# Retention's rotation split between two engines: GpSimd turns the queries, VectorE the keys

## The chip, the cores and the metric

One core of a Trainium2 chip runs the kernel. The core has five engines with instruction streams of their own (TensorE for matmuls, VectorE, ScalarE and GpSimd for elementwise work, SyncE for issuing transfers) and 16 DMA engines. They meet through semaphores only. The metric is the time of one execution on the device in microseconds; times within the trace count from the start of the span.

## The reference

The program is two blocks of two layers each, on 256 rows of width 1024. The second block is the one that matters here. In each of its layers the normalized rows are projected to queries, keys and values of a retention branch, to the features of an RWKV-7 branch (a recurrence over time, computed in chunks), to a pooling branch and to gates:

```python
def rotary(x, positions):
    half = x.shape[-1] // 2
    freqs = ROPE_BASE ** (-jnp.arange(half, dtype=jnp.float32) / half)
    ang = positions.astype(jnp.float32)[..., None] * freqs
    cos = jnp.cos(ang)[:, :, None, :]
    sin = jnp.sin(ang)[:, :, None, :]
    x32 = x.astype(jnp.float32)
    x1, x2 = x32[..., :half], x32[..., half:]
    return jnp.concatenate([x1 * cos - x2 * sin, x1 * sin + x2 * cos], axis=-1)
...
    qh = rotary(q.reshape(B, T, H, dh), positions)
    kh = rotary(k.reshape(B, T, H, dh), positions) * (dh ** -0.5)
...
    scores = jnp.einsum('bhnid,bhnjd->bhnij', qc, kc) * decay_mask[None, :, None]
```

With 4 heads of 128, both queries and keys are 256 rows of 512 numbers. The rotation is elementwise: each number is multiplied by a cosine and its partner by a sine, and the two products are subtracted or added.

## The kernel before

All weights stream through the core. Each projection is a piece of 128x2048 numbers, loaded by SyncE into a ring of three. ScalarE rounds a piece to its high half (`part0h` or `part1h`, two buffers in turn) and the low half (`part0l`, `part1l`) is the difference, made by VectorE for most pieces (line 1453, in two operations of 128x1024) and by GpSimd for some (line 3020). TensorE multiplies each piece in three passes, high by high, high by low and low by high, 48 matmuls for a projection, and waits for the first and for the second low half apart (`low_half`). The pieces of the second block go in the order `rw6 rw0 ... rw5 rq0 rq1 rk0 rk1 u0 u1 rv0 rv1 rg0 rg1 pg0 pg1 ...`, where `rq`, `rk` and `rv` are the retention's queries, keys and values, and `rg` its gate.

Nothing schedules at run time: each engine has its program in a written order. In a layer of the second block, `prepare` first does the features of the recurrence and then, from a list of jobs that all engines step through with `jobs.fill()`, the projections of the other branches between its own steps. On VectorE `prepare` ends with the scaled operands of the recurrence, `AR` (line 2257), `bt_` (line 2260) and the scaled keys `kt_` (line 2263), and then `jobs.fill()` makes the low half of `rg0`. On TensorE `prepare` turns (transposes) `vN` and `bkN` from these, multiplies `rg0`, does the pooling, waits for the signal `rot` and turns the rotated queries and keys (line 621).

The rotation before the change is GpSimd's: `rotate`, called behind the job `rk1`, runs over queries and keys and the two tiles of 128 rows. For each tile it makes four products of 128x256 into the tile `grow`, waits for them, and writes a difference and a sum back into the rows. `grow` later holds a gate row, which ScalarE writes behind the same signal `rot`.

Of the kernel before, what the change touches and what calls it, by code (L numbers as in the profile page):

```python
# [10 lines left out]
ALU = mybir.AluOpType  # L11
# [216 lines left out]
def v(ap, **k):  # L228
    names = list(k)
    return ap.rearrange("p (" + " ".join(names) + ") -> p " + " ".join(names), **{a: b for a, b in k.items() if b})  # L230
# [1207 lines left out]
def vector_program(w, K):  # L1438
    e, M, V, ps, at, done = w.e, K.mem, K.vector, K.psum, K.at, K.done
# [23 lines left out]
    def bank(*name):  # L1463
        w.wait_ge(*done[name if len(name) > 1 else name[0]])
        return ps[name]
# [706 lines left out]
    def headnorm_end(banks, name, n, d, dsts):  # L2172
# [7 lines left out]
            last = e.tensor_tensor(dst, dst, rv[:, k * n:k * n + n].unsqueeze(2).to_broadcast([128, n, d]), ALU.mult)  # L2180
        return last

    def prepare(l, jobs):
        Z = M.Z[l]
        V.mark("v", "begin", l)
# [8 lines left out]
        for j in (6, 0, 1, 2, 3, 4, 5):  # L2194
# [18 lines left out]
            if j == 4:  # L2213
                t = bank("ksum", l)
                e.tensor_scalar(Z.n8, t[0:8, 0:256], 1e-24, None, ALU.max).then_inc(*V("n8 in", l))
                ps.free(("ksum", l), V.now())
        for cp in range(2):
            t = bank("kn", cp, l)
# [42 lines left out]
        w.wait_ge(*at["kd", l])  # L2261
        w.wait_ge(*V.now())
        e.tensor_tensor(kt, k4, ee, ALU.mult).then_inc(*V("k", l))
        jobs.fill()
        V.mark("v", "ph2", l)
        jobs.fill()
# [2 lines left out]
        t = bank("pool", 1, l)  # L2269
        e.tensor_copy(Z.dT[:, 2:4, :], v(t[:, :], c=2, n=256)).then_inc(*V("dT", 1, l))  # L2270
        ps.free(("pool", 1, l), V.now())
        for i in range(2):
            t = bank("kT", i, l)
# [7 lines left out]
        for cp in range(2):  # L2281
            t = bank("bon", cp, l)
# [4 lines left out]
        for h in range(4):  # L2287
            t = bank("ST", h, l)
# [11 lines left out]
        for gp in range(2):  # L2300
            t = bank("pw", gp, l)
# [7 lines left out]
        for cp in range(2):  # L2309
            t = bank("yT", cp, l)  # L2310
# [169 lines left out]
    for l in range(L):  # L2480
        jobs = Jobs(jobs2(), lambda name: job2(l, name))
        prepare(l, jobs)
        norms = []
        for i in range(2):
            chunk(l, i, jobs, norms)
        turn_y(l, 1)
        V.mark("v", "end2", l)
        rwkv_low(l, 1)
        V.mark("A2", l, 0)
        V.mark("A2", l, 1)  # L2490
        jobs.rest()
        for j in range(4):
            merge(l, 2, j)
            if j == 1:
                split_to(PIECE[l, "out1"])
        for j in range(4):
            use(l, f"out{j}")
        for ch in range(2):
            combine(l, 0, ch)
        sum_squares(l + 1, 0)  # L2500
        if l < L - 1:
            scale_rows(l + 1, 0)
            split_to(PIECE[l + 1, "rw6"])
        combine(l, 1, 0)
        if l == L - 1:
            finish(0)
        combine(l, 1, 1)
        if l < L - 1:
            enter(l + 1)
# [495 lines left out]
def gpsimd_program(w, K):  # L3005
    e, M, G, ps, at, done, A, here = w.e, K.mem, K.gpsimd, K.psum, K.at, K.done, K.A, K.here
# [15 lines left out]
    def use(l, key):  # L3022
        split_to(ahead(PIECE[l, key]))

    def use_half(l, name):
        key, m = name.split(".")
        split_to(PIECE[l, key] + 1 + int(m))
# [93 lines left out]
        for q in "vs":  # L3121
            w.wait_ge(*at[q, what, l])

    def rotate(l):
        Z = M.Z[l]
        a, b = (v(M.grow[:, 512 * k:512 * k + 512], h=4, s=2, d=64) for k in range(2))
        w.wait_ge(*at["cs"])
        for src, n in ((Z.rq3, "rq"), (Z.rk3, "rk")):
            w.wait_ge(*at[n + "0", l])
            w.wait_ge(*at[n + "1", l])  # L3130
            for i in range(2):
                s4 = src[:, i, :].rearrange("p (h s d) -> p h s d", h=4, s=2)
                w.wait_ge(*G.now())
                for s in range(2):
                    e.tensor_tensor(a[:, :, s, :], s4[:, :, s, :], M.cs[:, 0, i, :].unsqueeze(1).to_broadcast([128, 4, 64]),
                                    ALU.mult).then_inc(*G())
                    e.tensor_tensor(b[:, :, s, :], s4[:, :, s, :], M.cs[:, 1, i, :].unsqueeze(1).to_broadcast([128, 4, 64]),
                                    ALU.mult).then_inc(*G())
                w.wait_ge(*G.now())
                e.tensor_tensor(s4[:, :, 0, :], a[:, :, 0, :], b[:, :, 1, :], ALU.subtract).then_inc(*G())  # L3140
                e.tensor_tensor(s4[:, :, 1, :], b[:, :, 0, :], a[:, :, 1, :], ALU.add).then_inc(*G("rot", l))

    def job2(l, name):
        if "." in name:
            use_half(l, name)
        else:
            use(l, name)
        if name == "rk1":
            rotate(l)

    def headnorm(nh, *name):
        w.wait_ge(*at["hvar", *name])
# [2 lines left out]
    for l in range(L):  # L3155
        Z = M.Z[l]
        jobs = Jobs(jobs2(), lambda name: job2(l, name))
        G.mark("g", "begin", l)
        if l == 0:
# [135 lines left out]
def build(nc, A, out):  # L3295
    with ExitStack() as ctx:
        K = Engines(nc, ctx, A, out)
        for program in (tensor_program, vector_program, scalar_program, gpsimd_program, sync_program):
            program(Port(Count()), K)
        K.at, K.done = ({k: a for k, a in t.items() if a[0] is not None} for t in (K.at, K.done))  # L3300
        K.restart()
        block = ctx.enter_context(nc.Block())

        @block.tensor
        def _(e):
            tensor_program(Port(e), K)

        @block.vector
        def _(e):
            vector_program(Port(e), K)  # L3310

        @block.scalar
        def _(e):
            scalar_program(Port(e), K)

        @block.gpsimd
        def _(e):
            gpsimd_program(Port(e), K)

        @block.sync  # L3320
        def _(e):
            sync_program(Port(e), K)
# [203 lines left out]
```

## Time and profile before

| | |
|---|---|
| median of 3 runs | 1578.39 us (1576.77, 1578.39, 1582.22) |
| the profiled execution | 1582.88 us |
| its span | 1581.0 us |
| mean granted TensorE clock | 0.996 |
| busy: TensorE, VectorE, ScalarE, GpSimd | 97%, 64%, 45%, 36% |

The span is what the profiler's records cover; the execution is 1.9 us longer. Busy shares are averages over the whole span, in which the four layers have different limits, and an engine that isn't the limit costs nothing by being idle. In the rows below, `Z` stands for the layer's own buffers (among them the retention's rows), `cs` for cosines and sines, `ps` for a PSUM bank.

### The profile page before, as it was taken

To read this page: it belongs to the slowest core of one execution; us is meant where nothing else is said; L and a number is where in the kernel's file an instruction comes from. 1 tells how busy PE (TensorE), PEld (TensorE's weight loads), DVE (VectorE), ACT (ScalarE), POOL (GpSimd) and SP (SyncE) were. 2 spreads that over 40 slices of the span, in tenths; PEclk is the share of its full clock that TensorE was granted. 3 is DMA by queue.
4 is the path that set the end of the run, shared out by engine and by line. 5 is a ranking of instruction groups with operands and counts; after the bars stand their busy time and mean duration, and the time that the engine had idled before them with its cause. 6 is when DMAs were issued, how large, how long until landed. Compare 5 with 4: busy or idle time off the path is not lost.

```text
span 1581.0 us, 35399 instructions
## 1 busy us (share of the span) xinstructions
PE 1538.2 (97%) x15704; PEld 1414.6 (89%) x15704; DVE 1005.7 (64%) x1637; ACT 712.1 (45%) x1126; POOL 563.0 (36%) x452
## 2 busy tenths in 40 slices
PE   9999999999999999999999999999999999999998
PEld 8989987899978989987999989999998899999887
DVE  4364386878784445576777786766446777764356
ACT  4554534544445455435444444633332555433223
POOL 3745613000217745503000310734673006446640
PEclk9999999999999999999999999999999999999999
DMA  9433364787545423474676545453333354533332
GB/s 357 169 122 108 113 232 191 265 299 273 187 166 211 161 89 125 161 279 187 250 283 240 204 142 182 152 176 133 135 136 135 124 197 153 182 133 138 114 130 93
DMA packets 43944, 281.49 MB, mean 178 GB/s; under 512 B 5144, under 2 KB 5272, under 8 KB 14352
## 3 DMA queue, kind: packets, MB, share of 16 engines
q1 hardware_dynamic: 42192, 270.13, 47.4%
q0 software_dynamic: 1600, 9.10, 1.5%
q8 instruction: 123, 2.02, 0.5%
q14 instruction: 29, 0.24, 0.0%
HBM read 278.15 MB, written 1.06 MB: 177 GB/s over the span
## 4 chain that ended last, share of the span: by engine, by line
PE 78%; DVE 13%; ACT 3%; issue 3%; POOL 2%; DMA 0%; POOLq 0%; SPq 0%; ACTq 0%; DVEq 0%
PE ps L613 75%; DVE part0l L1453 3%; DVE part1l L1453 3%; PE ps L621 3%; ACT part0h L2523 1%; DVE rows L1890 1%; ACT part1h L2523 1%; DVE Pr L1887 1%; ACT gates L2520 1%; ACT Xh L2523 1%; DVE Xl L1468 1%; DVE small L1484 0%; DMA ring<-in_w 0%; DVE raw L2012 0%; DVE mgx L2144 0%
## 5 line engine op out<-in xcount | busy, mean ns | idle before, releaser
L2523 ACT ACTIVATE part1h<-ring 128x1024 fp32r<-128x1024 f32 (+1 forms) x216 | 215.8, 1047 | 226.0 <-PE ps L613 213.6
L2523 ACT ACTIVATE part0h<-ring 128x1024 fp32r<-128x1024 f32 (+1 forms) x216 | 213.0, 1035 | 209.6 <-PE ps L613 194.3
L613 PE MATMUL ps<-Xh,part1h 128*128 128x256 f32 x968 | 276.7, 286 | 7.5 <-DVE Xl L1468 2.4
L613 PE MATMUL ps<-Xh,part0h 128*128 128x256 f32 (+1 forms) x952 | 270.9, 285 | 3.4 <-DVE Xl L1468 1.3
L613 PE MATMUL ps<-Xl,part1h 128*128 128x256 f32 x968 | 271.1, 280 | 0.0
L613 PE MATMUL ps<-Xh,part1l 128*128 128x256 f32 x968 | 270.9, 280 | 0.0
L613 PE MATMUL ps<-Xl,part0h 128*128 128x256 f32 (+1 forms) x952 | 265.2, 279 | 0.0
L613 PE MATMUL ps<-Xh,part0l 128*128 128x256 f32 (+1 forms) x952 | 265.1, 278 | 0.0
L3020 POOL TENSOR_TENSOR part1l<-ring,part1h 128x512 fp32r<-128x512 f32 x144 | 185.3, 1317 | 102.5 <-ACT part1h L2523 102.3
L3020 POOL TENSOR_TENSOR part0l<-ring,part0h 128x512 fp32r<-128x512 f32 x144 | 185.3, 1318 | 101.8 <-ACT part0h L2523 101.7
L1453 DVE TENSOR_TENSOR part1l<-ring,part1h 128x1024 fp32r<-128x1024 f32 (+1 forms) x144 | 181.3, 1299 | 52.3 <-ACT part1h L2523 52.0
L1453 DVE TENSOR_TENSOR part0l<-ring,part0h 128x1024 fp32r<-128x1024 f32 (+1 forms) x144 | 178.0, 1277 | 54.2 <-ACT part0h L2523 54.1
L613 PEld LDWEIGHTS ps<-Xh,part1h 128*128 128x128 f32 x968 | 183.7, 190 | 12.1 <-DVE Xl L1468 4.0
L613 PEld LDWEIGHTS ps<-Xh,part0h 128*128 128x128 f32 (+1 forms) x952 | 178.4, 187 | 7.9 <-DVE Xl L1468 2.3
L613 PEld LDWEIGHTS ps<-Xl,part1h 128*128 128x128 f32 x968 | 184.2, 190 | 1.1 <-issue 0.9
L613 PEld LDWEIGHTS ps<-Xh,part1l 128*128 128x128 f32 x968 | 183.8, 190 | 0.0
L613 PEld LDWEIGHTS ps<-Xl,part0h 128*128 128x128 f32 (+1 forms) x952 | 178.8, 188 | 1.6 <-issue 1.3
L613 PEld LDWEIGHTS ps<-Xh,part0l 128*128 128x128 f32 (+1 forms) x952 | 178.2, 187 | 0.0
L3058 POOL TENSOR_TENSOR x<-xh,rows 128x512 f32<-128x512 f32 x20 | 32.6, 1630 | 321.7 <-DVE hid L2002 284.5
L613 PE MATMUL ps<-part1h,Xh 128*128 128x256 f32 (+1 forms) x256 | 79.7, 311 | 2.9 <-DVE part1l L1453 2.3
L613 PE MATMUL ps<-part0h,Xh 128*128 128x256 f32 (+1 forms) x256 | 79.6, 311 | 2.3 <-DVE part0l L1453 1.7
L613 PE MATMUL ps<-part1l,Xh 128*128 128x256 f32 (+1 forms) x256 | 78.4, 306 | 0.0
(446 smaller groups left out, 3260.4 us busy)
## 6 DMA issues: line engine op xcount, KB each, us to landing
ring<-in_w SPq DMA_DIRECT2D x211, 1024.0 KB, 4.9
hid<-in_ada SPq DMA_DIRECT2D x36, 512.0 KB, 6.3
hid<-in_w SPq DMA_DIRECT2D x6, 1024.0 KB, 11.1
rows<-in_lnrow POOLq DMA_DIRECT2D x6, 1024.0 KB, 9.9
fqk<-in_ada SPq DMA_DIRECT2D x6, 512.0 KB, 6.1
cq<-in_ada SPq DMA_DIRECT2D x6, 512.0 KB, 6.5
gates<-in_c SPq DMA_DIRECT2D x2, 1536.0 KB, 9.5
ring<-in_w SPq DMA_DIRECT2D x4, 512.0 KB, 5.6
```

The costliest lines, as they stand in the source:

```text
L613: return e.matmul(o, a, b, start=st, stop=sp)
L621: return e.transpose(o, a, ident[0:a.shape[0], 0:a.shape[0]])
L1453: e.tensor_tensor(lo[:, h * c:h * c + c], raw[:, h * c:h * c + c], f32(hi[:, h * c:h * c + c]), ALU.subtract).then_inc(*V("low", m, h))
L1468: return e.tensor_tensor(hl[1], raw, f32(hl[0]), ALU.subtract).then_inc(*V(*name))
L1887: e.scalar_tensor_tensor(out=tmp, in0=g, scalar=1.0, in1=t[:, :], op0=ALU.add, op1=ALU.mult).then_inc(*V())
L1890: e.tensor_tensor(m, m, tmp, ALU.add).then_inc(*V("merged", bq, j, l))
L2520: return e.activation(o, a, f, **k)
L2523: return e.activation(o, a, ACT.Copy)
L3020: e.tensor_tensor(lo[:, o], raw[:, o], f32(hi[:, o]), ALU.subtract).then_inc(*G("low", m, h))
L3058: e.tensor_tensor(x3[:, i, c], xh3[:, i, c], M.rows[:, c], ALU.mult).then_inc(*G())
```

## The change

The rotation of the keys goes from GpSimd to VectorE. GpSimd's part, `rotate_queries`, is what `rotate` did for the queries, and ends with a signal of its own. VectorE's part, `rotate_keys`, stands directly behind the scaled keys (`kt_`) and ahead of the job that makes the low half of `rg0`. It waits for the queries first, since both use `grow`. It takes each product in one operation over 128x512 in place of two over 128x256, so a tile of rows needs 4 operations in place of 6, and it gives the signal `rot`.

```diff
@@ vector_program
+    def rotate_keys(l):
+        Z = M.Z[l]
+        a, b = (M.grow[:, 512 * k:512 * k + 512] for k in range(2))
+        a8, b8 = (t.rearrange("p (x d) -> p x d", d=64) for t in (a, b))
+        a4, b4 = (v(t, h=4, s=2, d=64) for t in (a, b))
+        w.wait_ge(*at["cs"])
+        w.wait_ge(*at["turned queries", l])
+        w.wait_ge(*at["rk0", l])
+        w.wait_ge(*at["rk1", l])
+        for i in range(2):
+            s8 = Z.rk3[:, i, :].rearrange("p (x d) -> p x d", d=64)
+            s4 = Z.rk3[:, i, :].rearrange("p (h s d) -> p h s d", h=4, s=2)
+            w.wait_ge(*V.now())
+            for t8, cs in ((a8, 0), (b8, 1)):
+                e.tensor_tensor(t8, s8, M.cs[:, cs, i, :].unsqueeze(1).to_broadcast([128, 8, 64]), ALU.mult).then_inc(*V())
+            w.wait_ge(*V.now())
+            e.tensor_tensor(s4[:, :, 0, :], a4[:, :, 0, :], b4[:, :, 1, :], ALU.subtract).then_inc(*V())
+            e.tensor_tensor(s4[:, :, 1, :], b4[:, :, 0, :], a4[:, :, 1, :], ALU.add).then_inc(*V("rot", l))
+
     def prepare(l, jobs):
...
         e.tensor_tensor(kt, k4, ee, ALU.mult).then_inc(*V("k", l))
+        rotate_keys(l)
         jobs.fill()
         V.mark("v", "ph2", l)
@@ gpsimd_program
-    def rotate(l):
+    def rotate_queries(l):
...
-        for src, n in ((Z.rq3, "rq"), (Z.rk3, "rk")):
-            w.wait_ge(*at[n + "0", l])
-            w.wait_ge(*at[n + "1", l])
-            for i in range(2):
-                s4 = src[:, i, :].rearrange("p (h s d) -> p h s d", h=4, s=2)
...
+        w.wait_ge(*at["rq0", l])
+        w.wait_ge(*at["rq1", l])
+        for i in range(2):
+            s4 = Z.rq3[:, i, :].rearrange("p (h s d) -> p h s d", h=4, s=2)
...
+            e.tensor_tensor(s4[:, :, 1, :], b[:, :, 0, :], a[:, :, 1, :], ALU.add).then_inc(*G("turned queries", l))
...
-        if name == "rk1":
-            rotate(l)
+        if name == "rk0":
+            rotate_queries(l)
```

VectorE in the first layer of the second block, from the scaled operands of the recurrence to the low halves of `rg0` and `rg1`, before:

```order
L2257 SCALAR_TENSOR_TENSOR AR<-gates,bt_ 128x8x128
L2260 TENSOR_TENSOR bt_<-kt_,Z 128x1024
L2263 TENSOR_TENSOR kt_<-gates,Z 128x1024
L1453 TENSOR_TENSOR part1l<-ring,part1h 128x1024 x2
L1453 TENSOR_TENSOR part0l<-ring,part0h 128x1024 x2
```

and after:

```order
L2276 SCALAR_TENSOR_TENSOR AR<-gates,bt_ 128x8x128
L2279 TENSOR_TENSOR bt_<-kt_,Z 128x1024
L2282 TENSOR_TENSOR kt_<-gates,Z 128x1024
L2197 TENSOR_TENSOR grow<-Z,cs 128x512 x2
L2199 TENSOR_TENSOR Z<-grow 128x4x64
L2200 TENSOR_TENSOR Z<-grow 128x4x64
L2197 TENSOR_TENSOR grow<-Z,cs 128x512 x2
L2199 TENSOR_TENSOR Z<-grow 128x4x64
L2200 TENSOR_TENSOR Z<-grow 128x4x64
L1453 TENSOR_TENSOR part1l<-ring,part1h 128x1024 x2
L1453 TENSOR_TENSOR part0l<-ring,part0h 128x1024 x2
```

Eight operations now stand between the scaled keys and the first low half of `rg0`; the rest of VectorE's order is the same.

GpSimd at the end of the rotation, the last tile of the keys and what follows it (a memset of the recurrence's masked scores), before:

```order
L3135 TENSOR_TENSOR grow<-Z,cs 128x4x64
L3137 TENSOR_TENSOR grow<-Z,cs 128x4x64
L3135 TENSOR_TENSOR grow<-Z,cs 128x4x64
L3137 TENSOR_TENSOR grow<-Z,cs 128x4x64
L3140 TENSOR_TENSOR Z<-grow 128x4x64
L3141 TENSOR_TENSOR Z<-grow 128x4x64
L3190 MEMSET Z 128x2048
```

and after, where it is the last tile of the queries:

```order
L3154 TENSOR_TENSOR grow<-Z,cs 128x4x64
L3156 TENSOR_TENSOR grow<-Z,cs 128x4x64
L3154 TENSOR_TENSOR grow<-Z,cs 128x4x64
L3156 TENSOR_TENSOR grow<-Z,cs 128x4x64
L3159 TENSOR_TENSOR Z<-grow 128x4x64
L3160 TENSOR_TENSOR Z<-grow 128x4x64
L3209 MEMSET Z 128x2048
```

The pattern is the same; it stands two times in a layer instead of four. The orders of TensorE, ScalarE and SyncE are unchanged.

## Rows read from the trace of the kernel before

**Rows 1.** Page, part 1: busy time of each engine, share and instructions.

```profile
PE 1538.2 (97%) x15704; PEld 1414.6 (89%) x15704; DVE 1005.7 (64%) x1637; ACT 712.1 (45%) x1126; POOL 563.0 (36%) x452
```

**Rows 2.** Page, part 4: engines' shares of the chain that ended last.

```profile
PE 78%; DVE 13%; ACT 3%; issue 3%; POOL 2%; DMA 0%; POOLq 0%; SPq 0%; ACTq 0%; DVEq 0%
```

**Rows 3.** Waits of TensorE, 945 to 1100: total us, times, longest.

```profile
PE ps L613 <- DVE part0l L1453: 1.5, 2, 1.0
PE ps L613 <- DVE part1l L1453: 0.6, 2, 0.4
```

**Rows 4.** Timeline of GpSimd, 925 to 1110: start, us, engine, line, what.

```profile
1005.69 1.52 POOL L3135 TENSOR_TENSOR grow<-Z,cs 128x256 f32<-128x256 f32 x1
...
1022.00 0.74 POOL L3141 TENSOR_TENSOR Z<-grow 128x256 f32<-128x256 f32 x1
1022.91 0.74 POOL L3135 TENSOR_TENSOR grow<-Z,cs 128x256 f32<-128x256 f32 x1 [0.17 <-POOL Z L3141]
...
1039.39 0.73 POOL L3141 TENSOR_TENSOR Z<-grow 128x256 f32<-128x256 f32 x1
```

**Rows 5.** Timeline of VectorE, 945 to 1100, around the scaled keys.

```profile
1024.00 3.11 DVE L1453 TENSOR_TENSOR part0l<-ring,part0h 128x1024 fp32r<-128x1024 f32 x2 [2.56 <-ACT part0h L2523]
1027.14 1.64 DVE L2257 SCALAR_TENSOR_TENSOR AR<-gates,bt_ 128x1024 f32<-128x1024 f32 x1
1028.82 1.65 DVE L2260 TENSOR_TENSOR bt_<-kt_,Z 128x1024 f32<-128x1024 f32 x1
1030.57 1.57 DVE L2263 TENSOR_TENSOR kt_<-gates,Z 128x1024 f32<-128x1024 f32 x1
1032.07 3.42 DVE L1453 TENSOR_TENSOR part1l<-ring,part1h 128x1024 fp32r<-128x1024 f32 x2
```

**Rows 6.** VectorE by line and shape: busy us, mean ns, idle before.

```profile
L1453 DVE TENSOR_TENSOR part1l<-ring,part1h 128x1024 fp32r<-128x1024 f32 x2 | 2.4, 1218 | 0.0
L2229 DVE TENSOR_TENSOR kt_<-bt_,gates 128x1024 f32<-128x1024 f32 x1 | 1.2, 1227 | 0.1
L2202 DVE TENSOR_TENSOR gates<-Z 128x512 f32<-128x512 f32 x6 | 4.2, 692 | 9.9 <-ACT Z L2523 9.9
L2220 DVE TENSOR_TENSOR bt_<-bt_,ps 128x512 f32<-128x512 f32 x2 | 1.3, 682 | 0.0
L2391 DVE TENSOR_TENSOR Z<-ps,c 128x256 f32<-128x256 f32 x2 | 0.8, 420 | 1.5 <-PE ps L613 1.5
```

**Rows 7.** Timeline of TensorE: the first matmuls of `rv1` and `rg0`.

```profile
1025.58 0.36 PE L613 MATMUL ps<-part0h,Xh 128*128 128x256 f32 x1 [0.99 <-DVE part0l L1453]
...
1033.96 0.36 PE L613 MATMUL ps<-Xh,part1h 128*128 128x256 f32 x1 [0.38 <-DVE part1l L1453]
```

**Rows 8.** The chain that ended last, 1000 to 1060: start, us, what.

```profile
1034.90 0.83 issue
1035.73 7.61 PE ps L613 x66
1043.35 1.75 PE ps L621 x16
```

**Rows 9.** Second layer: the chain at `rg0`; GpSimd's last operation.

```profile
1354.69 8.62 PE ps L613 x72
...
1360.13 0.73 POOL L3141 TENSOR_TENSOR Z<-grow 128x256 f32<-128x256 f32 x1
```

**Rows 10.** Timeline of TensorE: the first matmuls behind three long waits.

```profile
498.71 0.58 PE L613 MATMUL ps<-Xh,part1h 128*128 128x256 f32 x1 [2.27 <-POOL part1l L3020]
...
1217.61 0.36 PE L613 MATMUL ps<-A0h,part1h 128*128 128x256 f32 x1 [1.74 <-DVE A0l L1468]
...
1538.67 0.36 PE L613 MATMUL ps<-A1h,part0h 128*128 128x256 f32 x1 [1.94 <-DVE A1l L1468]
```

**Rows 11.** Stretches behind two of them: us, TensorE busy (matmuls), granted clock, DMA.

```profile
498.60:502.00 3.40, 3.29 (x15) 0.50 0.00 0
1217.60:1220.60 3.00, 2.99 (x26) 1.00 0.03 5
```

More of the change, by code:

```diff
@@ L3127, in rotate @@
         w.wait_ge(*at["cs"])
-        for src, n in ((Z.rq3, "rq"), (Z.rk3, "rk")):
-            w.wait_ge(*at[n + "0", l])
-            w.wait_ge(*at[n + "1", l])
-            for i in range(2):
-                s4 = src[:, i, :].rearrange("p (h s d) -> p h s d", h=4, s=2)
[L3133 to L3141, printed above, removed]
+        w.wait_ge(*at["rq0", l])
+        w.wait_ge(*at["rq1", l])
+        for i in range(2):
+            s4 = Z.rq3[:, i, :].rearrange("p (h s d) -> p h s d", h=4, s=2)
+            w.wait_ge(*G.now())
+            for s in range(2):
+                e.tensor_tensor(a[:, :, s, :], s4[:, :, s, :], M.cs[:, 0, i, :].unsqueeze(1).to_broadcast([128, 4, 64]),
+                                ALU.mult).then_inc(*G())
+                e.tensor_tensor(b[:, :, s, :], s4[:, :, s, :], M.cs[:, 1, i, :].unsqueeze(1).to_broadcast([128, 4, 64]),
+                                ALU.mult).then_inc(*G())
+            w.wait_ge(*G.now())
+            e.tensor_tensor(s4[:, :, 0, :], a[:, :, 0, :], b[:, :, 1, :], ALU.subtract).then_inc(*G())
+            e.tensor_tensor(s4[:, :, 1, :], b[:, :, 0, :], a[:, :, 1, :], ALU.add).then_inc(*G("turned queries", l))
     def job2(l, name):
```

## Prediction

> **What bounds the kernel now.** I read the page first. TensorE is busy 97% of the span [rows 1], and the chain that ended last is 78% TensorE and 13% VectorE [rows 2]. So only what makes TensorE wait, or slows it, can move the end. Next, the waits of TensorE around the retention of the first layer: 1.5 us for `part0l` and 0.6 us for `part1l` [rows 3]. These are the low halves of the split weights, which VectorE writes. No wait for GpSimd stands among them.
>
> Then GpSimd's own row of work. Its rotation runs from 1005.69 to 1040.12: 12 instructions for the queries to 1022.74, 12 for the keys from 1022.91 on [rows 4]. TensorE comes to the turning of the rows only at 1043.35 [rows 8], 3.2 us after the rotation's end. In the second layer the rotation ends at 1360.86 and the turning begins at 1363.31 [rows 9], 2.4 us later. The rotation's end is off the path in both layers; ending it earlier gives nothing by itself.
>
> What does stand on the path there is VectorE: `AR`, `bt_`, `kt_` and then the low half of `rg0`, one behind another from 1024.00 to 1035.49 [rows 5]. TensorE waited 0.99 us for the low half of `rv1` and 0.38 us for the first half of `rg0` [rows 7]. The change puts new work into exactly this row, ahead of the low half of `rg0`.
>
> **What it removes.** 12 GpSimd instructions a layer, 17.2 us of them [rows 4]. Nobody waits for them, so that alone is worth 0. But while they ran VectorE was slow: a 128x1024 operation with both inputs in SBUF took 1.64, 1.65 and 1.57 us and the pair for one piece 3.11 and 3.42 us [rows 5]; with GpSimd idle the same operation takes 1.227 us and the low half 1.218 each [rows 6], a pair about 2.36 us, since the second starts a little before the first ends. From 1022.74 on GpSimd will now be idle. So, from 1024.00: pair 2.36 instead of 3.11, three operations at 1.23 instead of 1.64, 1.65, 1.57. That is 0.75 + 0.41 + 0.42 + 0.34 = 1.9 us. `kt_` is ready at 1030.2 instead of 1032.1. The queries' rotation is not moved: the job in front of it now bears the name of another piece, but GpSimd comes to it at 1005.69 either way.
>
> The Trainium skill (SBUF — State Buffer, section Who interferes with whom) says that a VectorE instruction with two SBUF inputs contends with a GpSimd instruction that reads SBUF. By that rule the release is complete; the trace agrees, 1.227 us alone and about 1.65 us beside GpSimd.
>
> **What it adds.** Per layer 4 products of 128x512 and 4 sums of 128x256 on VectorE. A 128x512 of this kind takes 0.692 us, two in a row 1.28 us (0.682 each, overlapping), a 128x256 takes 0.42 us [rows 6], two about 0.8. With some 0.04 us for each wait on its own result (the distance from one operation to the next in rows 5) one tile of rows costs 0.04 + 1.28 + 0.04 + 0.82 = 2.2 us, both 4.4. The bounds: 4.0 if sums overlap fully, 5.7 if each ran as slowly as beside GpSimd (1.65/1.23 = 1.34 times). I take 4.4, since GpSimd is idle there. The new wait for the queries is open: they end at 1022.7, VectorE asks at 1030.2, so it costs 0 and has 7.5 us in hand. Queued behind the rotation on VectorE are the low halves of `rg0` and `rg1`. For the first TensorE waits; the second is needed 6 us later and is hidden behind `rg0`'s 48 matmuls, as now.
>
> **The sum.** Rotation from 1030.3 to 1034.7; the first low half of `rg0` 1.23 us, to 1035.95; TensorE starts 0.14 us behind it, near 1036.1. Before it started at 1033.96 [rows 7]: 2.1 us later. Two things take some back. In the first layer TensorE stood another 0.83 us without an engine to blame, within `rg0` [rows 8]; I count it as fetching of instructions, which the longer wait will cover: 2.1 - 0.8 = 1.3 us. In the second layer no such gap stands [rows 9], but the second low half came 1.71 us behind the first (half of 3.42 us), while its 12 first matmuls take 1.4 us (26 in 3.00 us [rows 11]); now it comes 1.13 us behind and is in time: 2.1 - 0.3 = 1.8 us. Together 3.1 us, bounds 1.5 (rotation 4.0, gaps wholly covered) and 6 (rotation 5.7, nothing covered).
>
> **What the longer wait does to TensorE's clock.** TensorE ends its small matmuls for `vN` and `bkN` at 1033.6 now (0.38 us ahead of 1033.96 [rows 7]), and at 1033.2 then, for `rv1` starts 0.35 us earlier. From there to 1036.1 it will stand 2.9 us, in each layer; no wait of this trace is that long. The two longest are 2.27 us and 1.94 us [rows 10]. Right behind the first the granted clock was 0.50 for 3.40 us: 15 matmuls, against 26 in 3.00 us at 1.00 behind a wait of 1.74 us [rows 10, 11]. Fifteen matmuls at the full rate take 1.73 us, so the fall from 2.4 to 1.2 GHz cost 3.40 - 1.73 = 1.7 us; a little less if part of it falls within the wait. I take 1.6 us. Bounds: 0 (no fall, as behind 1.74 us) to 3.4 (it lasts twice as long). Waits of 2.9 us lie beyond the ones that brought the fall, so I expect it in both layers: 3.2 us.
>
> The Trainium skill (TensorE: Matmul & The Clock Gate, section What's actually happening) has it that the throttled state is the default and activity releases it, so that an idle TensorE goes back to 1.2 GHz. By that rule both waits end in the low clock; the trace agrees at 2.27 us, and at 1.74 us it shows no fall.
>
> **Total.** 3.1 + 3.2 = 6.3 us. The profiled execution took 1582.88 us (span 1581.0 and 1.9 around it), so a like one of the changed kernel comes to 1589.2. The median of the runs shown is 4.5 us below the profiled one; the change adds the same to it: 1578.4 + 6.3 = 1584.7 us. What a measurement of this kernel can tell from no change is about 0.3%, 4.7 us.
>
> **Rivals.**
> 1. The waits come but the clock falls in one layer only or in none. For it: 1.74 us left the clock up, and where a fall begins is not the kernel's to choose. Against: 2.9 us is well above both waits that had it. Price 3.1 to 4.7 us: 1581.5 to 1583.1, mostly within 0.3%.
> 2. VectorE isn't given back its speed, because something other than GpSimd made it slow (the transfers of that stretch). Then `kt_` stays at 1032.1, the rotation ends at 1036.6 and TensorE waits 4 us a layer: 1.9 x 2 = 3.8 us more than my sum, 1588.5. Against: the same kind of operation is at 1.227 us 15 us later, once GpSimd is idle [rows 6].
> 3. Not slower, rather a little faster: the release outweighs the rotation. TensorE's waits of 0.99 and 0.38 us in each layer and the 0.83 us gap were born of VectorE's slow stretch; if all went it would be 0.99 + 0.38 + 0.83 + 0.99 + 0.38 = 3.6 us, 1574.8. The one mechanism is a rotation short enough to fit into what GpSimd gives back: it decides below about 1.5 us between `kt_` and the low half (1.9 us won, 0.4 lost to TensorE's readiness). For it: VectorE wins 1.9 us ahead and another 1.1 us (3.42 to 2.36) behind. Against: 8 instructions cannot be under 4.0 us by rows 6, and what is won behind the low half of `rg0` comes too late for it.
> 4. The change shortens a path that I think is open, TensorE's wait for the rotated rows. It would be 5 us earlier (1040.1 to 1034.7), but TensorE is not there before 1043: no gain, and the rest of my sum remains. If the late low half were then taken up by a later wait, the time would be 1578 to 1580. Against: no later wait of that stretch is for anything but VectorE's work behind TensorE itself.
>
> **How the numbers follow.** Forecast 0.55; rival 1 0.27; rival 2 0.08; rival 3 0.05; rival 4 0.05. Slower by over 0.3%: the forecast with 6.3 us lies 1.6 us above the bound, and I give it 0.85 of its chance, 0.47; of rival 1 a quarter, 0.07; rival 2, 0.08; together 0.62. Faster by over 0.3% needs 4.7 us, more than rival 3's whole price; I leave 0.03 to it for the scatter of the runs. Within 0.3%: 0.35. The range: the low end below rival 1 without a fall by what three runs scatter (they span 5.4 us), 1578.5; the high end at rival 2 without going beyond it, 1588.5. The forecast's own range is 1582.5 to 1587.
>
> **What would show it.** Right: on VectorE `AR`, `bt_` and `kt_` at 1.23 us each and `kt_` ending near 1030.2; 8 instructions of rotation in 4.4 us behind it; TensorE waiting about 2.9 us for the low half of `rg0` in both layers; the granted clock at 0.50 for some 3.4 us right behind; GpSimd idle from 1022.7 to its memset behind 1052; the turning of the rows still not waiting for the rotation. Wrong: a wait of TensorE below 1.5 us there (rotation or release mis-sized), a clock that stays at 1.00 (then 3 us), VectorE at 1.65 us without GpSimd beside it, or TensorE waiting less elsewhere by what it waits more here.

## The result, and the profile after

The changed kernel takes 1583.72 us (median of 15 runs, 1581.92 to 1587.72), the kernel before 1579.05 us in the same comparison (15 runs, 1575.59 to 1582.22). The ratio is 1.003, with a 95% interval of 1.0022 to 1.0038: 4.7 us slower, and clear of no change. The forecast was 6.3 us slower and 1584.7 us. The profiled execution of the changed kernel took 1583.84 us, only 1.0 us more than that of before: the clock fell at other places in the one than in the other (near 1482 and 1540 before, near 12 and 1036 after), so traces are compared stretch by stretch, and times by medians.

The timeline of VectorE in the changed kernel, first layer, from `rv1`'s low half (columns: start, us, engine, line, what; compare [rows 5]):

```profile
1023.16 2.36 DVE L1453 TENSOR_TENSOR part0l<-ring,part0h 128x1024 fp32r<-128x1024 f32 x2 [2.56 <-ACT part0h L2543]
1025.55 1.22 DVE L2276 SCALAR_TENSOR_TENSOR AR<-gates,bt_ 128x1024 f32<-128x1024 f32 x1
1026.81 1.23 DVE L2279 TENSOR_TENSOR bt_<-kt_,Z 128x1024 f32<-128x1024 f32 x1
1028.14 1.22 DVE L2282 TENSOR_TENSOR kt_<-gates,Z 128x1024 f32<-128x1024 f32 x1
1029.47 1.29 DVE L2197 TENSOR_TENSOR grow<-Z,cs 128x512 f32<-128x512 f32 x2
1030.80 0.42 DVE L2199 TENSOR_TENSOR Z<-grow 128x256 f32<-128x256 f32 x1
1031.14 0.42 DVE L2200 TENSOR_TENSOR Z<-grow 128x256 f32<-128x256 f32 x1
...
1033.60 2.35 DVE L1453 TENSOR_TENSOR part1l<-ring,part1h 128x1024 fp32r<-128x1024 f32 x2
```

This whole trace stands 0.84 us earlier here than that of before. From the start of `rv1`'s low half to the end of `kt_` it is 6.20 us now and was 8.14: GpSimd's retreat gave 1.9 us. Between `kt_` and `rg0`'s low half the rotation puts 4.2 us.

GpSimd's timeline, the last operation of the queries and the next one ([rows 4] went on to 1040.12):

```profile
1021.16 0.74 POOL L3160 TENSOR_TENSOR Z<-grow 128x256 f32<-128x256 f32 x1
1053.94 1.80 POOL L3209 MEMSET Z<- 128x2048 f32 x1 [32.04 <-PE ps L613]
```

TensorE's first matmul of `rg0` in the first and in the second layer, to be read against [rows 7]:

```profile
1034.96 0.36 PE L613 MATMUL ps<-Xh,part1h 128*128 128x256 f32 x1 [2.50 <-DVE part1l L1453]
...
1358.45 0.36 PE L613 MATMUL ps<-Xh,part0h 128*128 128x256 f32 x1 [2.70 <-DVE part0l L1453]
```

0.38 us of waiting in each layer has become 2.50 and 2.70. The gap of 0.83 us within `rg0` [rows 8] is gone: the chain has all matmuls from `rg0` to the turning as one piece (start, us, what):

```profile
1033.68 1.15 DVE part1l L1453
1034.83 0.14 issue
1034.96 10.00 PE ps L613 x72
1044.96 1.75 PE ps L621 x16
```

And the granted clock, in stretches ahead of and behind both waits (length, busy us and count of TensorE, of its weight loads, VectorE, ScalarE, GpSimd, then clock, DMA share, GB/s):

```profile
1032.50:1034.90 2.40, 0.00 (x0) 0.00 (x0) 2.37 (x5) 2.40 (x5) 0.00 (x0) 1.00 0.64 265
...
1036.50:1039.00 2.50, 2.50 (x14) 2.50 (x13) 1.72 (x2) 0.00 (x0) 0.00 (x0) 0.50 0.78 242
...
1358.50:1362.00 3.50, 3.50 (x31) 3.50 (x32) 3.21 (x3) 0.32 (x1) 0.00 (x0) 1.00 0.42 114
```

Behind the wait of the first layer the clock fell to 1.2 GHz, 14 matmuls in 2.50 us; behind that of the second it stayed at 2.4 GHz.

To compare traces I use one distance: from VectorE's start on `rv1`'s low half to TensorE's start on the turning. It holds all that the change does between, and no fall elsewhere.

| kernel | first layer | second layer |
|---|---|---|
| before | 19.18 us | 18.42 us |
| changed | 21.64 (clock fell) | 20.03 |
| difference | +2.46 | +1.61 |

### The profile page after: what moved, and what is told of

Read it like the earlier page. It is cut to its first block, busy times and chain, and to the rows that moved or that the text cites. A ratio compares the mean times of both kernels' runs of the same rounds, so it can differ in the third digit from the quotient of the medians.

```text
span 1581.9 us, 35389 instructions
## 1 busy us (share of the span) xinstructions
PE 1535.9 (97%) x15704; PEld 1413.7 (89%) x15704; DVE 1005.9 (64%) x1653; ACT 712.1 (45%) x1126; POOL 529.4 (33%) x428
## 4 chain that ended last, share of the span: by engine, by line
PE 77%; DVE 14%; ACT 4%; issue 3%; POOL 2%; DMA 0%; POOLq 0%; SPq 0%; DVEq 0%; ACTq 0%
PE ps L613 75%; DVE part0l L1453 3%; DVE part1l L1453 3%; PE ps L621 3%; ACT part0h L2543 1%; DVE rows L1890 1%; DVE mgx L2144 1%; ACT part1h L2543 1%; ACT Xh L2543 1%; DVE Xl L1468 1%; DVE Pr L1887 1%; ACT gates L2540 1%; DVE mt L2140 0%; DVE small L1484 0%; DMA ring<-in_w 0%
## 5 line engine op out<-in xcount | busy, mean ns | idle before, releaser
L613 PE MATMUL ps<-part0l,Xh 128*128 128x256 f32 (+1 forms) x256 | 78.4, 306 | 0.0
```

Of the source, the lines that this page charges most:

```text
L613: return e.matmul(o, a, b, start=st, stop=sp)
```

## The experiments

Each edit is to the changed kernel unless another is named.

**The rotation behind the low half of `rg0`.**

```diff
         e.tensor_tensor(kt, k4, ee, ALU.mult).then_inc(*V("k", l))
-        rotate_keys(l)
         jobs.fill()
+        rotate_keys(l)
```

> The keys' rotation stays on VectorE, but stands behind the low half of rg0 instead of ahead of it. Theory (the rotation costs because it stands in the row that ends in rg0's low half): TensorE no longer waits there, also not the 0.38 us of before, and the clock does not fall; about 1.2 us in the first layer and 0.7 us in the second are won against before: 1577 us, 6 to 7 us below the changed kernel. Rival (what counts is the work added to VectorE, 4.2 us a layer, wherever it stands): 1582 to 1584 us, and TensorE waits somewhere else, for the low half of rg1 or for the rotated rows.

Measured: 1578.38 us, before 1578.87, ratio 0.9999 (0.999 to 1.0009). VectorE's timeline in it, first layer:

```profile
1029.30 1.23 DVE L2282 TENSOR_TENSOR kt_<-gates,Z 128x1024 f32<-128x1024 f32 x1
1030.44 2.35 DVE L1453 TENSOR_TENSOR part1l<-ring,part1h 128x1024 fp32r<-128x1024 f32 x2
1032.90 1.29 DVE L2197 TENSOR_TENSOR grow<-Z,cs 128x512 f32<-128x512 f32 x2
...
1036.69 0.42 DVE L2200 TENSOR_TENSOR Z<-grow 128x256 f32<-128x256 f32 x1
1037.03 2.35 DVE L1453 TENSOR_TENSOR part0l<-ring,part0h 128x1024 fp32r<-128x1024 f32 x2
```

The same 8 operations cost nothing against before here, so the place was what cost 4.7 us, not the work; the rival is out. The rotation ends at 1037.1 and TensorE turns at 1042.51. The distance is 18.19 and 17.30 us, 1.0 and 1.1 us below before (expected were 1.2 and 0.7); yet the median doesn't show 2 us, only 0 with an interval of some 1.5 us to either side. The executions of this kernel lost more to the lower clock than those of before (5.6 us against 4.5 by their mean granted clocks, with a standard error of 0.9 on the difference; the section on the prediction says how this is reckoned). That may be half of it, and it is not settled.

**No rotation of the keys.**

```diff
         e.tensor_tensor(kt, k4, ee, ALU.mult).then_inc(*V("k", l))
-        rotate_keys(l)
         jobs.fill()
@@ rotate_queries
-            ... ALU.add).then_inc(*G("turned queries", l))
+            ... ALU.add).then_inc(*G("rot", l))
```

> The keys are not rotated at all (this part of the computation is left out); the queries' rotation stays on GpSimd and everything else as in the changed kernel. It prices the rotation: the changed kernel minus this is the whole cost of the 8 VectorE operations a layer. Theory: 1576.5 to 1577.5 us, below before by the waits of 0.38 us and what else VectorE's slow stretch cost; a rotation that is hidden must come to this time. Rival (freeing GpSimd wins nothing): 1579 us as before.

This kernel leaves out a part of the computation; it only prices it. Measured: 1578.73 us, ratio 1.0003 (0.9993 to 1.0012), the same within the noise as with the rotation behind `rg0`'s low half: there it is hidden. I had expected about 2 us less than before. One reason stands in TensorE's timeline, within `rg0` of the first layer:

```profile
1031.67 0.28 PE L613 MATMUL ps<-Xh,part1l 128*128 128x256 f32 x1
1034.32 0.28 PE L613 MATMUL ps<-Xh,part1h 128*128 128x256 f32 x1 [2.37 <-issue]
```

The gap of 0.83 us of before is 2.37 us here, though VectorE had written all of the low half by 1030.22. Time won ahead of `rg0` was given back in it. The last experiment takes this up.

**GpSimd kept busy with reads.** Behind the queries it makes 12 more operations of the rotation's shapes, which read the turned queries.

```diff
         if name == "rk0":
             rotate_queries(l)
+            Z = M.Z[l]
+            a, b = (v(M.mt[:, 512 * k:512 * k + 512], h=4, s=2, d=64) for k in range(2))
+            for i in range(2):
+                s4 = Z.rq3[:, i, :].rearrange("p (h s d) -> p h s d", h=4, s=2)
+                ...  # 4 products of s4 with M.cs into a and b, a difference and a sum within a
```

> The changed kernel, and GpSimd goes on behind the queries with 12 instructions of the shapes of the keys' rotation that read the turned queries and write to a buffer that nothing reads. Theory (GpSimd's reads make VectorE slow): AR, bt_ and kt_ back at about 1.6 us, kt_ 1.9 us later, the rotation on VectorE 5.5 to 6 us instead of 4.1, TensorE waits 5.5 to 6.5 us for rg0's low half in each layer, 1590 to 1594 us. Rival (the release had another cause): VectorE stays at 1.23 us and the time at 1583 to 1585 us.

Measured: 1597.38 us, ratio 1.0122 (1.0108 to 1.0135). VectorE's timeline:

```profile
1028.74 1.65 DVE L2279 TENSOR_TENSOR bt_<-kt_,Z 128x1024 f32<-128x1024 f32 x1
1030.49 1.57 DVE L2282 TENSOR_TENSOR kt_<-gates,Z 128x1024 f32<-128x1024 f32 x1
1032.16 2.18 DVE L2197 TENSOR_TENSOR grow<-Z,cs 128x512 f32<-128x512 f32 x2
1034.38 0.83 DVE L2199 TENSOR_TENSOR Z<-grow 128x256 f32<-128x256 f32 x1
```

`bt_` and `kt_` take 1.65 and 1.57 us, as before the change. The rotation takes 6.9 us from 1032.16 on, more than the 5.5 to 6 expected: the short operations suffer most, 0.83 us against 0.42. TensorE waits 6.78 us in each layer, and the time lies 3 us above the expected range.

**GpSimd kept busy with writes.**

```diff
         if name == "rk0":
             rotate_queries(l)
+            for _ in range(20):
+                w.wait_ge(*G.now())
+                e.memset(M.mt, 0.0).then_inc(*G())
```

> The changed kernel, and GpSimd goes on behind the queries with 20 memsets of 128x1024 into a buffer that nothing reads, each behind the other: it writes all through VectorE's row from 1023 to 1034, but reads nothing. Theory (only GpSimd instructions that read SBUF slow VectorE's operations with two inputs): AR, bt_ and kt_ stay at 1.22 us, the products at 1.29 us for two, time as the changed kernel, 1582 to 1587 us. Rival (any GpSimd instruction does): 1.6 us each and TensorE waits 5 us and more for rg0's low half.

Measured, one run: 1579.96 us. GpSimd and, in the same stretch, VectorE and TensorE:

```profile
1020.95 20.18 POOL L3171 MEMSET mt<- 128x1024 f32 x20
...
1025.80 1.23 DVE L2279 TENSOR_TENSOR bt_<-kt_,Z 128x1024 f32<-128x1024 f32 x1
1027.13 1.22 DVE L2282 TENSOR_TENSOR kt_<-gates,Z 128x1024 f32<-128x1024 f32 x1
1028.46 1.29 DVE L2197 TENSOR_TENSOR grow<-Z,cs 128x512 f32<-128x512 f32 x2
...
1033.95 0.36 PE L613 MATMUL ps<-Xh,part1h 128*128 128x256 f32 x1 [2.50 <-DVE part1l L1453]
```

GpSimd is as busy as in the experiment before and VectorE isn't slowed at all. What slows VectorE is GpSimd's reading, as the Trainium skill has it (SBUF — State Buffer, section Who interferes with whom: a GpSimd instruction that only writes does not contend with one of VectorE that has two SBUF inputs). The time is below the 1582 expected; in this execution the clock fell behind neither wait (2.50 us in both layers), and the distance is 20.0 us in both. The chain (start, us, what) has the 72 matmuls from `rg0` to the turning of the first layer in 8.37 us, where the changed kernel's took 10.00, so the fall there cost 1.6 us:

```profile
1033.95 8.37 PE ps L613 x72
1042.33 1.75 PE ps L621 x16
```

**The rotation made twice.** The second time it writes to a buffer that nothing reads.

```diff
+        m4 = v(M.mt[:, 0:512], h=4, s=2, d=64)
+        for i in range(2):
+            ...  # the same two products of Z.rk3 into a and b
+            e.tensor_tensor(m4[:, :, 0, :], a4[:, :, 0, :], b4[:, :, 1, :], ALU.subtract).then_inc(*V())
+            e.tensor_tensor(m4[:, :, 1, :], b4[:, :, 0, :], a4[:, :, 1, :], ALU.add).then_inc(*V("rot", l))
```

> The changed kernel with the keys' rotation made a second time into a buffer that nothing reads: 16 operations on VectorE ahead of rg0's low half. Theory (everything ahead of that low half is on the path): 4.2 us later in each layer, TensorE's wait 6.7 to 6.9 us instead of 2.5 and 2.7, the clock falls in both layers, 1592 to 1596 us. Rival (TensorE's wait has another cause, and VectorE has room): wait and time as the changed kernel.

Measured, one run: 1594.02 us. TensorE's first matmul of `rg0` and the clock around it (columns as above):

```profile
1039.20 0.55 PE L613 MATMUL ps<-Xh,part1h 128*128 128x256 f32 x1 [6.74 <-DVE part1l L1453]
```

```profile
1036.00:1039.00 3.00, 0.00 (x0) 0.00 (x0) 2.96 (x6) 0.00 (x0) 0.00 (x0) 0.50 0.00 0
1039.20:1045.00 5.80, 5.80 (x27) 5.80 (x28) 3.26 (x3) 0.00 (x0) 0.00 (x0) 0.50 0.66 230
```

4.24 us more of VectorE, 4.24 us more of waiting: one to one. Here the clock fell within the wait and was down through the 5.8 us shown behind it, 27 matmuls in place of 50. It fell in both layers, as in both layers of the experiment with reads; the 72 matmuls from `rg0` on took 11.26 and 9.94 us in place of 8.37, so these falls cost 2.9 and 1.6 us.

**TensorE given work in its wait.** Twice, with another number of plain fp32 matmuls whose result nothing reads (n = 20, then 5):

```diff
         turn_heads(l, "bkN", [t[:, :, 0:128] for t in (M.bt, M.kt)])
+        keep_busy(n)
```

> The changed kernel, with 20 matmuls of 128x256 into an unread bank put in front of rg0 in each layer, so that TensorE works through most of its wait of 2.5 to 2.7 us (20 x 0.116 = 2.3 us). Theory (about one execution in two has the clock fall behind each of these waits, 1.6 us each): no fall there, granted clock 1.00 behind the wait, median 1.0 to 2.5 us lower, 1581 to 1582.7 us, and a narrower spread. Rival (the falls come elsewhere as often): median as the changed kernel, 1583 to 1584.5 us, mean clock the same.

Measured with 20: 1600.04 us, ratio 1.0133 (1.012 to 1.0147). This tells nothing of the question: the matmuls took 9.2 us.

> The changed kernel with 5 unread matmuls in front of rg0 in each layer. The first try with 20 of them took 9.2 us instead of the 2.3 us reckoned with, since these are plain fp32 matmuls at 0.46 us each and not the kernel's rounded ones at 0.12 us; 5 of them take 2.3 us and fit the wait of 2.5 to 2.7 us. Theory (the wait itself costs about 3 us in all, and the clock falls behind it add 1.6 us each, a little more than one in an execution): no fall behind them, granted clock 1.00 there, 1581 to 1582.7 us. Rival (no more falls at these places than elsewhere): 1583 to 1584.5 us.

Measured with 5: 1581.09 us, before 1577.95, ratio 1.0015 (1.0005 to 1.0026). Behind the filled waits:

```profile
1038.00:1042.00 4.00, 4.00 (x37) 4.00 (x36) 1.68 (x2) 0.00 (x0) 0.00 (x0) 1.00 0.87 305
1359.30:1363.00 3.70, 3.70 (x33) 3.70 (x34) 3.19 (x3) 0.51 (x1) 0.00 (x0) 1.00 0.44 135
```

3.1 us above before, where the changed kernel is 4.7 above: some 1.6 us of the change's cost goes when TensorE has work in the wait, which is the price of one fall. The two intervals overlap a little (1.0022 to 1.0026), so the share is likely and not certain. Nor is the filling clean. In the first layer of the profiled execution TensorE stood within the added matmuls (the trace has two records for each) and began `rg0` at 1037.81, 1.4 us after VectorE's low half allowed it:

```profile
1033.90 1.78 PE L613 MATMUL ps<-cg 128*128 128x256 f32 x7
1037.25 0.92 PE L613 MATMUL ps<-cg 128*128 128x256 f32 x3 [1.57 <-issue]
```

Where that happens, the filling gives back less than the fall costs.

**Both rotations on VectorE.** GpSimd rotates nothing; the 16 operations stand behind `rg0`'s low half.

```diff
@@ vector_program
+    def rotate_rows(l):
+        ...  # as rotate_keys, without the wait for "turned queries", in a loop:
+        for src, n in ((Z.rq3, "rq"), (Z.rk3, "rk")):
+            ...
@@ prepare
-        rotate_keys(l)
         jobs.fill()
+        rotate_rows(l)
@@ gpsimd_program
-        if name == "rk0":
-            rotate_queries(l)
```

> The queries' rotation goes to VectorE too, in the same form, and both stand behind the low half of rg0; GpSimd rotates nothing. Theory: VectorE is no longer slowed from 1005 on, so TensorE's waits of 0.22, 0.48 and 0.8 us in each layer go or shrink; the 8.3 us of rotation end near 1039 to 1040 and the turning begins near 1041, with no wait. 2.5 to 3.5 us below the same with the keys alone (1578.4 us): 1575 to 1576 us, 3 to 4 us below before. Rival (16 operations are too many for the room on VectorE between the low half of rg0 and the turning): TensorE waits 1 to 3 us for the rotated rows or the low half of rg1, 1577 to 1581 us.

Measured: 1574.86 us, before 1577.95, ratio 0.9979 (0.9969 to 0.9989). This is the fastest version, 3.1 us below before by the medians (3.3 by the ratio) and about 0.5% below the changed kernel, by their ratios to before. TensorE's waits in it from 940 to 1100, where before had those of [rows 3]:

```profile
PE ps L613 <- issue: 2.9, 2, 1.7
PE ps L613 <- DVE Xl L1468: 0.3, 1, 0.3
PE ps L613 <- DVE part1l L1453: 0.2, 1, 0.2
```

Of the 2.1 us for low halves of weights, 0.2 is left; but 1.7 of the 2.9 us that no engine explains lies within `rg0`.

**The same without a load.** To the kernel with both rotations on VectorE:

```diff
-        load("late", M.late, A["c2"][:, C2O["dm"][0]:C2N], "late", l)
+        if l:
+            load("late", M.late, A["c2"][:, C2O["dm"][0]:C2N], "late", l)
```

(and the two waits for it likewise). That layer's decay masks and pooling matrices are then not there.

> The kernel with both rotations on VectorE, with the load of the decay masks and pooling matrices (1.5 MB, in flight from 1024.5 on) left out in the first layer of the second block; that layer's masks are then wrong, which changes no duration. In it TensorE stood 1.68 us within rg0 (0.83 before, 0.56 with the keys behind rg0's low half, 2.37 without the keys) though VectorE's low half had long been written. Theory (its instructions are fetched by the same transfer engines, which that load and the next piece keep busy): the gap shrinks to under 0.5 us, and some 1.5 us is won. Rival (the gap is a matter of TensorE's own queue at this place of the program): it stays at 1 to 2.4 us.

Measured, one run: 1576.98 us, before 1580.75 beside it. TensorE's waits from 940 to 1100:

```profile
PE ps L613 <- issue: 1.1, 1, 1.1
PE ps L613 <- DVE Xl L1469: 0.2, 1, 0.2
PE ps L613 <- DVE part1l L1454: 0.2, 1, 0.2
```

The gap within `rg0` is gone; one of 1.1 us further on is left. It is one execution against one, which can't tell whether the 1.5 us are won: 3.8 us below before, where both rotations on VectorE alone gave 3.1.

Nor does the load explain the gap by itself. The second layer issues the same load, and no kept trace has such a gap there. The kernel without the keys' rotation had 2.37 us in the first layer; four microseconds around the same place in both layers (columns as above: TensorE's busy time comes first, the DMA share is the last but one):

```profile
1031.00:1035.00 4.00, 1.63 (x16) 1.54 (x13) 1.80 (x2) 3.11 (x5) 0.00 (x0) 1.00 0.98 401
1350.00:1354.00 4.00, 4.00 (x145) 3.80 (x145) 1.91 (x2) 2.75 (x6) 0.00 (x0) 1.00 0.90 318
```

With the load in flight and the DMA engines nearly as busy, TensorE ran through. So the gap went with the load in one execution, and something of the first layer must come to it. That instructions of TensorE are fetched late is my reading; the trace names no cause, and it stays open.

## Why the prediction was right, and where it was too high

- **What bounds that stretch.** Right. The wait that mattered was TensorE's for `rg0`'s low half; it grew one to one with what was put ahead of it on VectorE (2.50 us, then 6.74), and the same work behind that low half was free.
- **The release.** Forecast 1.9 us, measured 1.9. The experiments with reads and with writes show that it is GpSimd's reading that slows VectorE; rival 2 is out. One argument against rival 2 was misread: the operation of 1.227 us [rows 6] ran at 996.5, ahead of the rotation and not 15 us behind it. Another of that size, at 1046.91, took 1.23 us, so the argument stands.
- **The rotation.** Forecast 4.4 us, measured 4.2: 1.29 us for two products, 0.42 for a sum, which overlapped a little more than I had reckoned.
- **The wait.** Forecast 2.9 us, measured 2.50 and 2.70. Part is the rotation's 0.2 us; the rest is the low half (0.1 us less than taken) and TensorE's small matmuls, which ended 0.1 us later than I had them. Without a fall the stretch is 1.6 us longer in the second layer (forecast 1.8) and 0.8 in the first (the 20.0 us of the kernel with memsets, less 19.18; forecast 1.3): 2.4 us for the 3.1 of the sum.
- **The gap of 0.83 us.** Right that the longer wait covers it. But I took it as a fixed 0.83 us; without a wait it was 0.56, 1.7 and 2.4 us in three kernels, and took from two of them part of what they should win. That it is fetching of instructions was not shown.
- **The clock: this term was too large.** "I expect it in both layers: 3.2 us". The price of one fall was right (1.6 us). Its frequency was not: in two profiles of waits of 2.50 to 2.70 us (the changed kernel and the one with memsets) it fell in one of four. The measured 4.7 us less 2.4 leave 2.3 us for it, 1.4 falls an execution, and filling the waits took away 1.6 us, about one. Rival 1 thus describes part of the executions.

  The granted clock of every execution says the same. At half clock TensorE takes twice as long, so (1 - mean clock) x span is about what the lower clock cost. In the mean, with its standard error, that is 4.2 ± 0.3 us for the kernel before (44 executions of the later comparisons), 6.7 ± 0.6 for the changed one (15) and 4.7 ± 0.5 with the waits filled (12): the change adds 2.4 ± 0.7 us, for the 3.2 of the forecast. With both rotations on VectorE it is 5.6 ± 0.6, 1.7 above before in the same comparison, so that version gained more in its stretches than its median shows.

  I had taken the length of a wait for what decides, on two cases that had the fall. The three waits of [rows 10], near 499, 1217 and 1538 us, come in all eleven traces, with slightly different lengths. The lower clock followed none of ten of 1.64 to 1.74 us, nine of twelve of 1.92 to 1.94 us and five of eleven of 2.17 to 2.28 us; with one of four at 2.50 to 2.70 us, length alone does not decide it. Near 1482 in the trace of before it even fell behind 1.42 us. The wait of 2.27 us that my price rests on had it; in the kernel without the keys' rotation the same wait, again 2.27 us, had not.
- **The total.** Being only 1.0 us off 1584.7 is in part luck: the difference was forecast 1.6 us too large, and the three runs of before that I added it to stood 0.7 us below the median of fifteen.
- **Rivals 3 and 4.** Out: no rotation was short enough to fit, and TensorE never waited for the rotated rows.

## What to carry to other kernels

In these runs, work moved onto an engine off the bound was free or cost its full length, by where it stood in that engine's order: look for what is queued behind it and who waits for that. Here one line's place made 4.7 us, and moving the whole rotation behind the awaited product turned a loss of 0.3% into a gain of 0.2%. When GpSimd is idle beside VectorE, count what it gives back, but ask whether it gives back ahead of the wait or behind it.

## What the runs showed of the hardware

- VectorE with two SBUF inputs beside GpSimd: 1.23 us alone or beside memsets, 1.65 us beside reads. A short operation (128x256) went from 0.42 to 0.83 us.
- At five places of the program, over eleven traces, the lower clock followed waits of TensorE of 1.64 to 1.74 us in none of ten cases, of 1.92 to 1.94 us in nine of twelve, of 2.17 to 2.28 us in five of eleven and of 2.50 to 2.70 us in one of four; at 6.74 to 6.78 us it came in four of four, beginning within the wait. One fall cost 1.6 us behind the shorter waits, 1.6 to 2.9 us behind the longest.
- A plain fp32 matmul of 128x256 took 0.46 us, where the rounded ones of this kernel take 0.12 us.
- TensorE stood 0.56 to 2.37 us at one place of its program in the first layer, in four kernels, as idle time without a releaser. It did not in one execution without a load of 1.5 MB in flight there, and not in the second layer, where the same load is in flight; the cause is open.
